# A decoder step on one core: written-out projection groups, moved stores and products, a second output buffer in the experts

## The reference

```python
def decoder_layer(x, c, conv_buf, h0, attend, p):
    mod = (jax.nn.silu(c) @ p['w_ada'] + p['b_ada'])[:, None, :]
    shift1, scale1, gate1, shift2, scale2, gate2 = jnp.split(mod, 6, axis=-1)
    xn = rms_norm(x, p['norm_mix']) * (1 + scale1) + shift1
    q, k, v, xr, yb = jnp.split(xn @ p['w_in'], [512, 1024, 1536, 2048], axis=-1)
    attn = rms_norm(attend(q, k, v, p['sb_bias']), p['norm_attn'])
    xc, conv_new = causal_conv(xr, conv_buf, p['conv_w'], p['conv_b'])
    h, h_last = rg_lru(xc, h0, p['rg_wa'], p['rg_ba'], p['rg_wx'], p['rg_bx'], p['rg_lambda'])
    rg = rms_norm(h * jax.nn.gelu(yb), p['norm_rg'])
    x = x + gate1 * (jnp.concatenate([attn, rg], axis=-1) @ p['w_out'])
    xn2 = rms_norm(x, p['norm_ffn']) * (1 + scale2) + shift2
    x = x + gate2 * hier_moe(xn2, ...)
    return x, k, v, conv_new, h_last

# attend, per head: z = q.k / 8 + bias;  A[t,s] = sigmoid(z_ts) * prod_{s<j<t} (1 - sigmoid(z_tj)), s < t;  out = A @ v
# hier_moe: the best of 4 groups of 8 experts, in it the top 2; each expert is (silu(x @ w1) * (x @ w3)) @ w2, 1024 -> 512 -> 1024
```

## Time and profile before

| | |
|---|---|
| median of the runs | 3350.25 us |
| the profiled execution's own time | 3343.97 us |
| its span in the trace | 3342.5 us |
| mean granted clock of TensorE in it | 0.929 of full speed |
| TensorE busy | 2733.3 us (82%) |
| VectorE busy | 1389.8 us (42%) |
| GpSimd busy | 1001.9 us (30%) |
| ScalarE busy | 904.4 us (27%) |
| moved by DMA | 576 MB, 172 GB/s over the span |

### The profile page before, as it was taken

How to read it: one execution, slowest core, us unless ns; L and a number is a source line. 1 busy time by engine, 2 the same in 40 slices (tenths; PEclk the granted TensorE clock), 3 DMA queues, 4 the chain that set the end, 5 groups by cost and what they waited for, 6 DMA issues and landing times. The chain is left out here.

```text
span 3342.5 us, 46087 instructions
## 1 busy us (share of the span) xinstructions
PE 2733.3 (82%) x15013; PEld 1394.1 (42%) x15013; DVE 1389.8 (42%) x2262; ACT 904.4 (27%) x1684; POOL 1001.9 (30%) x1006
## 2 busy tenths in 40 slices
PE   5989898956777777678776899959999999899960
PEld 2444444422444444344442344435544544455530
DVE  1232313125888888633322577631111121121129
ACT  1313130304677767522222121111000000000014
POOL 0101010103878878723333133321111111111124
PEclk8999999978999999899988899979999999999985
DMA  7020201038140620199996533366686767967538
GB/s 281 13 75 13 75 13 75 13 110 313 53 133 11 184 63 1 59 311 341 335 341 223 166 123 132 107 238 216 228 288 205 236 217 261 348 230 254 171 106 340
DMA packets 277752, 576.43 MB, mean 172 GB/s; under 512 B 61222, under 2 KB 77671, under 8 KB 273368
## 3 DMA queue, kind: packets, MB, share of 16 engines
q1 hardware_dynamic: 195348, 429.56, 37.0%
q0 software_dynamic: 81952, 145.17, 13.2%
q10 hardware_dynamic: 324, 0.10, 0.0%
HBM read 462.96 MB, written 111.50 MB: 172 GB/s over the span
## 5 line engine op out<-in xcount | busy, mean ns | idle before, releaser
L1919 PE MATMUL h<-w,xT 128*64 128x256 f32 x5120 | 594.9, 386 | 0.7 <-ACT xT L1895 0.7
L909 POOL TENSOR_TENSOR w<-take,left 128x512 f32<-128x512 f32 (+3 forms) x320 | 484.8, 1544 | 116.7 <-DVE left L966 80.7
L966 DVE TENSOR_TENSOR_SCAN left<-leave,left 128x512 f32<-128x512 f32 (+3 forms) x320 | 454.4, 1447 | 77.9 <-ACT leave L940 77.5
L1919 PEld LDWEIGHTS h<-w,xT 128*64 128x64 f32 x5120 | 364.1, 138 | 222.1 <-issue 52.1
L407 PE MATMUL bank<-xnT,w_in 128*128 128x512 f32 x768 | 337.4, 602 | 28.3 <-DVE xnT L508 28.3
L1932 PE MATMUL yb<-w,hT 128*64 128x512 f32 x1280 | 314.6, 613 | 0.0
L1004 PE MATMUL tb<-ident,w 128*128 128x128 f32 x1088 | 174.2, 284 | 126.6 <-DVE wT L922 123.7
L1900 ACT ACTIVATE sg<-h 128x128 f32<-128x128 f32 x160 | 44.3, 277 | 729.8 <-PE h L1919 729.8
L407 PEld LDWEIGHTS bank<-xnT,w_in 128*128 128x128 f32 x768 | 148.4, 194 | 214.9 <-issue 185.7
L1869 POOL DMA_DIRECT2D x_in<-xs_d x162 | 85.2, 530 | 498.3 <-PE xb L1911 481.3
L1592 PE MATMUL pb<-w_out,featT 128*128 128x512 f32 x512 | 226.4, 595 | 0.8 <-DVE t L1657 0.8
(11 more groups left out here) (362 smaller groups left out, 3101.5 us busy)
## 6 DMA issues: line engine op xcount, KB each, us to landing
w<-in_w SPq DMA_DIRECT2D x96, 2048.0 KB, 21.8
vp<-in_cache_v POOLq DMA_DIRECT2D x256, 256.0 KB, 5.0
w<-in_cache_k SPq DMA_DIRECT2D x256, 256.0 KB, 4.9
ys_d<-zeros SPq DMA_DIRECT2D x32, 800.0 KB
slab<-in_w_ada SPq DMA_DIRECT2D x24, 1024.0 KB, 13.5
ys_d<-y POOLq DMA_DIRECT2D x82, 256.0 KB, 9.4
x_in<-xs_d POOLq DMA_DIRECT2D x162, 128.0 KB
x_t<-in_x_prompt SPq DMA_DIRECT2D x5, 2048.0 KB, 7.7
```

The source lines that it names most:

```text
L909: pool.tensor_tensor(w[n % 4][:, 0:cols], take[n % 4][:, 0:cols], left[n % 4][:, at + 1:at + cols + 1], ALU.mult).then_inc(s_w, 1)
L966: dve.tensor_tensor_scan(left[n % 4][:, at:at + cols][:, ::-1], leave[n % 4][:, 0:cols][:, ::-1], leave[n % 4][:, 0:cols][:, ::-1], left[n ...
L1919: mm = pe.matmul(h[half][q * G:q * G + G, 0:2 * P], xT[:, c % (XW // P), c // (XW // P) * G:c // (XW // P) * G + G], w13[i][:, c, :, cols] ...
```

## The change

In the **modulation**, the load of `x_t` moves ahead of the slabs, and the sample rows' load, norm, transposes and products move here from the sample projection (new tile `xnT_s`, which lives on and later holds `oT_new` and `rgT_new`). In the **projection**, the loops of all engines are written out in four groups, so that register waits become constant ones; `xr0` waits for each transposed chunk by itself; the last group loads and norms nothing ahead; the last convolution rows and the last state go to two small tiles that outlive the phase. The five **scattered stores** from these go out on GpSimd's queue at the start of the sample projection and are waited for at its end. In **prompt attention**, the product moves from GpSimd to VectorE, one item behind the scan; VectorE keeps the copies of every fourth item (80), ScalarE takes 240; there are three banks `tb`, and the two output banks share one. In the **experts** there are two `y`, written by turns, one more store ahead of the first (all rows of `ys_d` move up by 64, so the router's multiplier and `Y_PIECE` change), and GpSimd waits before each store for all stores before it. In the **closing stage**, `x1` is not loaded tile by tile: SP fetches it at the end of the experts into weight slots whose experts are done, and `yy` and `out` lie in other slots.

```diff
 def modulation_phase(nc, io, keep, sems):
+                sp.dma_start(x_t[:, :, :], io["x_prompt"][0].rearrange("(g j p) n -> g p j n", j=TPG, p=P)[0]).then_inc(s_x, 16)
+                sp.dma_start(x_s[:, :], io["x_sample"].rearrange("b t n -> (b t) n")).then_inc(s_xs, 16)
                 for c in range(KC):
                     sp.dma_start(slab[c][:, :], w_ada[c, :, 0:4 * 512]).then_inc(s_slab[c], 16)
-                    if c == 3:
-                        sp.dma_start(x_t[:, :, :], io["x_prompt"][0].rearrange("(g j p) n -> g p j n", j=TPG, p=P)[0]).then_inc(s_x, 16)
...
+                act.activation(junk[0:NS, :], x_s[:, :], ACT.Square, scale=1.0 / math.sqrt(D), accum_out=ssq_s[:, 0:1])
...
+                for c in range(KC):
+                    mm = pe.transpose(ps_x[:, c * NS:c * NS + NS], x_s[:, c * P:c * P + P], ident[0:NS, 0:NS])
...
 def projection_phase(nc, io, keep, sems):
-                with pe.Fori(0, NGRP) as g:
+                for g in range(NGRP):
...
                         for i, (w, m) in enumerate(parts):
+                            if name == "xr0":
+                                wait_out(pe, f"xT{i}", g)
                             mm = pe.matmul(ps[:, :], w, m, start=(i == 0), stop=(i == len(parts) - 1))
...
-                    for c in range(KC):
-                        wait_out(pe, f"xT{c}", g)
...
-                    for f in range(FC):
-                        sp.dma_start(conv_o[f], xr[:, f, 0:CONV - 1]).then_inc(s_tail, 16)
-                    sp.dma_start(io["h_prompt"][0].rearrange("a (f p) -> p (a f)", p=P), h_last[:, :]).then_inc(s_tail, 16)
-                for s, n in ((st_q, NGRP), (st_v, NGRP), (st_k, NGRP), (st_kT, NGRP), (st_rg, NGRP), (s_tail, FC + 1), (s_x, NGRP)):
-                    sp.wait_ge(s, 16 * n)
+                sp.wait_ge(st_q, 16 * NGRP)
...
 def sample_projection_phase(nc, io, keep, sems):
             def _(pool):
+                    for f in range(FC):
+                        pool.dma_start(conv_o[f], keep["conv_tail"][:, f, :]).then_inc(s["tail"], 16)
+                    pool.dma_start(io["h_prompt"][0].rearrange("a (f p) -> p (a f)", p=P), keep["h_tail"][:, :]).then_inc(s["tail"], 16)
...
                 pool.wait_ge(s["ri"], 32)
+                pool.wait_ge(s["tail"], 16 * FC + 16)
...
 def prompt_attention_phase(nc, io, keep):
-        tb = [k.ps(f"tb{i}", [P, GRP]) for i in range(2)]
-        ob = [k.ps(f"ob{i}", [P, 512]) for i in range(2)]
+        tb = [k.ps(f"tb{i}", [P, GRP]) for i in range(3)]
+        ob = k.ps("ob", [P, 2, 2 * P])
...
-                    pool.tensor_tensor(w[n % 4][:, 0:cols], take[n % 4][:, 0:cols], left[n % 4][:, at + 1:at + cols + 1], ALU.mult).then_inc(s_w, 1)
...
-                return s_ca if n % 2 else s_cd
+                return s_ca if n % 4 else s_cd
...
+                    dve.tensor_tensor(w[n % 4][:, 0:cols], take[n % 4][:, 0:cols], left[n % 4][:, at + 1:at + cols + 1], ALU.mult).then_inc(s_w, 1)
...
+                    if n:
+                        weights(n - 1)
-                    if n >= LAG and n % 2 == 0:
+                    if n >= LAG and n % 4 == 0:
                         turned(dve, dve.tensor_copy, n - LAG)
...
 def experts_phase(nc, io, keep, sems):
-        y = k.sb("y7", [P, XW])
+        y = k.sb("y7", [P, 2, XW])
...
+                hold(sp, s["y"], sp.snap(done, min_val=1, max_val=MAX_BLOCKS), s["sp"])
+                sp.dma_start(keep["x1_a"], x1_rows[:, 0:8, :]).then_inc(sems["x1_a"], 16)
+                sp.dma_start(keep["x1_b"], x1_rows[:, 8:12, :]).then_inc(sems["x1_b"], 16)
...
+                pool.dma_start(strips(io["ys_d"], 0), y[:, 0, :]).then_inc(s["st"], 16)
...
                     hold(pool, s["ye"], n + 1, s["sp"])
-                    pool.dma_start(strips(io["ys_d"], n * G), y[:, :]).then_inc(s["st"], 16)
+                    hold(pool, s["st"], 16 * n + 16, s["sp"])
+                    pool.dma_start(strips(io["ys_d"], n * G + G), y[:, ds(n & 1, 1), :].rearrange("p a n -> p (a n)")).then_inc(s["st"], 16)
...
-                    dve.tensor_copy(y[:, :], yb[:, :])
+                    dve.tensor_copy(y[:, ds(n & 1, 1), :].rearrange("p a n -> p (a n)"), yb[:, :])
...
 def final_phase(nc, io, keep, sems):
-                def load(i):
-                    sp.dma_start(x1[i % SETS][0:size[i], :], io["x1_d"][row0[i]:row0[i] + size[i], :]).then_inc(s_x[i % SETS], 16)
```

More of the change, by code:

```diff
@@ L454, in _ @@
                 act.nop().then_inc(s_xn, 1)
-                with act.Fori(0, NGRP) as g:
+                for g in range(NGRP):
                     for f in range(FC):
@@ L484, in _ @@
                     values(0, 2)
-                    norm(g + 2)
+                    if g + 1 < NGRP:
+                        norm(g + 2)
                     values(2, TPG)
@@ L503, in inverse @@
                     dve.reciprocal(rstd[:, :], ssq[:, :]).then_inc(s_rs, 1)
-                with dve.Fori(0, NGRP) as g:
+                for g in range(NGRP):
                     for c in range(KC):
@@ L562, in _ @@
             def _(pool):
-                with pool.Fori(0, NGRP) as g:
+                for g in range(NGRP):
                     wait_out(pool, f"yb{FC - 1}", g)
@@ L637, in _ @@
             def _(pool):
+                with nc.allow_non_contiguous_dma(reason="a few thousand bytes"):
+                    conv_o = io["conv_prompt"][0, 0].rearrange("j (f p) -> f p j", p=P)
+                    for f in range(FC):
+                        pool.dma_start(conv_o[f], keep["conv_tail"][:, f, :]).then_inc(s["tail"], 16)
+                    pool.dma_start(io["h_prompt"][0].rearrange("a (f p) -> p (a f)", p=P), keep["h_tail"][:, :]).then_inc(s["tail"], 16)
                 b_ada = io["b_ada"]
@@ L680, in _ @@
             def _(pe):
-                pe.wait_ge(s["xn"], 1)
-                for c in range(KC):
-                    mm = pe.transpose(ps["x"][:, c * NS:c * NS + NS], x_s[:, c * P:c * P + P], ident[0:NS, 0:NS])
-                mm.then_inc(s["xT"], 1)
-                pe.wait_ge(s["xnT"], 1)
                 for c in range(KC):
@@ L1958, in _ @@
             def _(dve):
-                dve.memset(y[:, :], 0.0)
+                dve.memset(y[:, :, :], 0.0)
                 dve.drain().then_inc(s["go"], 1)
@@ L1991, in final_phase @@
         f_row = k.sb("f_row", [P, D])
-        x1 = [k.sb(f"x1_8{i}", [P, D]) for i in range(SETS)]
-        yy = [k.sb(f"yy{i}", [P, 2, D]) for i in range(SETS)]
-        out = [k.sb(f"out8{i}", [P, D]) for i in range(SETS)]
+        x1 = [keep["x1_s"]] + [keep["x1_a" if t < 8 else "x1_b" if t < 12 else "x1_c"][:, t % 4 + 4 * (4 <= t < 8), :] for t in range(NT)]
+        yy = [keep["yy"][:, 2 * i:2 * i + 2, :] for i in range(SETS)]
+        out = [keep["w2_0"][:, i, :] for i in range(SETS)]
         junk = k.sb("junk8", [P, D], BF16)
@@ L1997, in final_phase @@
         s = {n: k.sem(f"p8_{n}") for n in ("f", "g0", "sum", "x2", "sq", "out")}
-        s_x = [k.sem(f"p8_in{i}") for i in range(SETS)]
         s_y = [k.sem(f"p8_y{i}") for i in range(SETS)]
```

180 lines of the change are left out of this document (94 added, 86 removed).

## The result

The changed kernel took 3248.7 us in the median of four runs (3245.06 to 3254.69), beside 3353.29 us for the kernel before (3349.2 to 3356.95). The ratio is 0.969, with a 95% interval of 0.967 to 0.9711. The forecast was 3238 us with a range of 3190 to 3288. The profiled execution took 3248.32 us at a span of 3246.9 us, 95.6 us less than before; the sum had forecast 112 less. The total is near, but the large terms miss in both directions.

A forecast was written before the change was run, and what follows sets the result against it. No engine was taken to bound the kernel throughout: VectorE was busiest in prompt attention, TensorE in the experts, both with waits. Terms of +0.4, -17, -19, -23, -55 and +2 gave about -112, from 3350.25 to 3238 us; range 3190 to 3288.

The forecast's parts named there:

- Modulation, +0.4: Modulation: moving the sample rows in and the load of x_t ahead costs 0.4 us, for one more 128 KB load.
- Projection, -17: Projection: TensorE waiting chunk by chunk at group starts, with loops written out, gains 17 us; bounds 10 and 22.
- Between the stages, -19: Between projection and sample projection: no longer waiting there for five scattered stores gains 19 us; bounds 8 and 21.
- hold the slabs up as long: Rival, sample projection: the scattered stores delay the slab loads equally, so the 19 us stay; 3257 us, chance 0.06.
- Attention, -23: Prompt attention: products on VectorE, copies 80 to 240 and three transpose banks gain 23 us; VectorE becomes the bound.
- slower: Rival, prompt attention: scans stay at 1634 ns without GpSimd's products and products stretch alike; 3387 us, chance 0.05.
- Read port rule: Rival, prompt attention: VectorE and GpSimd share a read port, so moving the product gains nothing; 3285 us, chance 0.12.
- Experts, -55: Experts: two output buffers keep single late stores from reaching TensorE, gaining 55 us; bounds 10 and 75.
- about 17 us stay, and I say 20: Experts: of 75 us lost, about 20 remain, from the store chain's 947 us against TensorE's 930.
- has a whole block to spare: Experts: the next x_in load, queued behind GpSimd's wait on stores, has a whole block of time to spare.
- the stores bind: Rival, experts: the store chain keeps TensorE late at one- or two-block experts, only 15 us return; 3278 us, chance 0.15.
- The rest, +2: Remaining edits cost 2 us: extra store, larger memset and end waits about +3, closing stage -1; bounds -4 and +8.

## Why the prediction was right, and where it was not

The sum of the terms: forecast -112 us, measured -95.6 in the profiled execution.

- **Modulation, +0.4.** Right: the projection's first instruction on VectorE stands at 47.16 us for 46.93.
- **Projection, -17.** The mechanism is right, as the run with all eight waits shows; the chunk waits were worth 21.65 us, near the upper bound of 22 that was named for the case that no matmul is slow any more. The few tenths of the written-out loops don't show; the projection's last store went out 20.05 us earlier.
- **Between the stages, -19.** The wait that left the stage's head gave 19.0 us, as the step said. What failed is the sentence that the five scattered stores "beside the slabs" cost "about 1 us": they cost 15.3 us, and with the 2.6 us that the rest of the head gave (0.8 in the estimate), 12.7 of the gain went back. That sentence had no row under it; the row that could have warned is the 17.1 us that one store of 2 KB took to land. The rival that they "hold the slabs up as long" came true in that part.
- **Attention, -23.** Right in its mechanism: the scan fell to 1.28 us, VectorE became the bound. Two terms were mis-sized. The products took 188 us for 196; and the overlap was taken at 0.065 us an instruction, where it was (357.9 + 187.9 + 46.2 - 533.4) / 720 = 0.081, what the earlier trace rows gave for copies back to back. VectorE was busy 533 us for the 553 forecast, its gaps were 19 us for 16 (first scan 774.9, last 1326.0), and so the stage gained 38.7 us, inside the bounds of -24 and 52. Against the rival *slower*, the prediction said that no scan of full length is listed alone in this stage; 18 were in its trace, at 1283 to 1285 ns.
- **Read port rule.** By the Trainium skill, page "Perfetto Trace Analysis", section "Optimizing Scalar/DVE Operations", moving the product between the two engines might not help. Here it helped by 21 us, with most copies off VectorE. That the two engines disturb each other the trace bears out (1841 ns a scan with GpSimd computing, 1279 without), and this is why it paid: the product left the engine that disturbed the scan.
- **Experts, -55.** Half as much. The step that failed is "about 17 us stay, and I say 20" of 75: 41.5 us stay in the intervals. The chain's need was set against TensorE's as totals, 947 against 930 us; but 21.8 of the 41.5 us stand in six intervals from 2735 to 2827, where three experts in a row have one block each, and 8.9 in the stage's first two. Slack gathered elsewhere can't be saved for them: one buffer holds one block. The step that the next `x_in` load "has a whole block to spare" failed in nine places, where the load landed behind the store that was issued just ahead of it. The rival *the stores bind* named this mechanism and place, with only 15 us coming back; 28 came back, between it and the forecast.
- **The rest, +2.** The first block starts 7 us later, 5 of them by the store ahead of the first load, which the run with 2 KB in its place shows to be worth nothing by itself. The closing stage gained 3.1 us (100.2 for 103.3) where 1 was forecast; no run undoes its edits.

So the total was close in part by luck: attention and the projection gave 19 us more than forecast and the closing stage 2, while the scattered stores and the experts, with the store ahead of the first, gave some 36 less. Which part of the store chain's landing time is due to weights in flight was not tried apart.

## What to carry to other kernels

A transfer that is moved off a wait and beside other transfers is not hidden: look at what shares its DMA engines, and move it to a stage that has room. That holds for a load behind a store as well: an issue in time is no landing in time. When a chain of waits is set against an engine, compare them over the stretch where the chain is longest, not as totals; here the second buffer took up single late stores, but not a run of them. When an elementwise step moves between VectorE and GpSimd, add the other engine's slower instructions to the price.

## What the runs showed of the hardware that was not expected

- Five stores of 8 KB in all, by their access patterns 2048 single words of 4 bytes, held the traffic beside them to 108 GB/s over 15 us, where it was 358 without them, at a mean busy share of the DMA engines of 1.07.
- A scan on VectorE took 1841 ns beside products on GpSimd and 1279 ns with none, 44% more; with fewer instructions on VectorE it was slower still than the 1634 ns before.
- A load of 2 x 128 KB issued 2 to 6 us behind a store of 256 KB on the same queue landed 1.4 to 2.2 us behind that store, 10.7 to 14.6 us after its issue, in the nine places where TensorE waited for it.
- Moving the loads ahead of the stores made the stage 44 us longer (2140.74 to 3187.80, 1047.1 for 1003.0): the order in one queue cost more than the late loads.
